# Retention scales one step later, next projections bank by bank, four row reads from GpSimd, router tables behind the first reload

## The reference, cut to what matters

```python
def first_block(x, ...):
    xn = rmsnorm(h, attn_norm_g[l])
    proj = xn @ w_in[l]
    q_da, k_da, v_da, q_r, k_r, v_r, g_r = jnp.split(proj, IN_SPLITS, axis=-1)
    o_da = diff_attention(...)
    o_r = retention(q_r, k_r, v_r, g_r)
    h = h + jnp.concatenate([o_da, o_r], axis=-1) @ w_out[l]
    xn = rmsnorm(h, ffn_norm_g[l])
    h = h + hier_moe(xn, router_group_w[l], router_group_b[l], ...)
    ...

def retention(q, k, v, g):
    s = jnp.einsum('bnchd,bnshd->bnhcs', qc, kc) * intra_decay
    intra = jnp.einsum('bnhcs,bnshe->bnche', s, vc)
    kv = jnp.einsum('bnshd,hs,bnshe->bnhde', kc, k_decay, vc)
    def step(state, kv_n):
        return state * chunk_decay + kv_n, state
    ...
    cross = jnp.einsum('bnchd,hc,bnhde->bnche', qc, q_decay, prev)
    o = head_rmsnorm(intra + cross)
    o = jax.nn.silu(g) * o

def conformer_conv(x, w_in, b_in, conv_w, conv_b, ln_g, ln_b, w_out, b_out):
    a, g = jnp.split(x @ w_in + b_in, 2, axis=-1)
    h = a * jax.nn.sigmoid(g)
    h = lax.conv_general_dilated(h, conv_w[:, None, :], ..., padding=[(30, 0)],
                                 feature_group_count=D_MODEL) + conv_b
    h = jax.nn.silu(layer_norm(h, ln_g, ln_b))
    return h @ w_out + b_out
```

## Time and profile before

| | us |
|---|---|
| median of 3 runs | 2126.69 |
| lowest, highest | 2125.68, 2127.67 |
| the profiled execution | 2125.95 |
| its span, from first to last instruction | 2124.1 |
| TensorE busy | 1962.6 (92% of the span) |
| VectorE, ScalarE, GpSimd busy | 1600.2, 1056.4, 542.0 |
| mean granted TensorE clock | 0.971 |

### The profile page before, as it was taken

One profiled execution on the slowest core, in us unless ns is written; L12 is line 12 of the kernel. 1 busy time (PEld: TensorE's weight loads), 2 busy tenths in 40 slices (PEclk: granted clock), 3 DMA queues, 4 the chain that ended last, 5 costly groups with the idle time before them and its releaser, 6 DMA issues. The chain is left out here.

```text
span 2124.1 us, 30096 instructions
## 1 busy us (share of the span) xinstructions
PE 1962.6 (92%) x11159; PEld 1057.4 (50%) x11159; DVE 1600.2 (75%) x1704; ACT 1056.4 (50%) x1396; POOL 542.0 (26%) x343
## 2 busy tenths in 40 slices
PE   6988988889499999999995899949999999999999
PEld 5775446644345544445442556534544444444444
DVE  6855637753789999999997746575697888889876
ACT  5332326731368888888875546474332323232320
POOL 2221131000023333333320001012002665557530
PEclk9999999999799999999997999979999999999999
DMA  6111320033289999999997446437101112121111
GB/s 243 41 41 40 109 60 1 1 135 127 78 328 416 403 421 404 404 398 395 407 366 303 162 161 225 148 109 287 40 1 55 65 40 79 39 79 39 61 58 80
DMA packets 80980, 363.69 MB, mean 171 GB/s; under 512 B 13993, under 2 KB 27945, under 8 KB 48313
## 3 DMA queue, kind: packets, MB, share of 16 engines
q1 hardware_dynamic: 61704, 309.64, 37.2%
q0 software_dynamic: 18640, 52.53, 7.3%
q10 hardware_dynamic: 544, 0.26, 0.0%
HBM read 337.21 MB, written 37.75 MB: 177 GB/s over the span
## 5 line engine op out<-in xcount | busy, mean ns | idle before, releaser
L432 PE MATMUL ps<-split,xt 128*128 128x512 f16 (+1 forms) x776 | 290.6, 374 | 5.2 <-issue 4.6
L649 DVE SCALAR_TENSOR_TENSOR split<-stage,split 128x2048 f16<-128x2048 f32 x128 | 289.5, 2282 | 5.6 <-ACT split L645 3.8
L433 PE MATMUL ps<-split,xt 128*128 128x512 f16 (+1 forms) x776 | 290.5, 374 | 0.0
L434 PE MATMUL ps<-split,xt 128*128 128x512 f16 (+1 forms) x776 | 290.2, 374 | 0.0
L645 ACT ACTIVATE split<-stage 128x2048 f16<-128x2048 f32 x128 | 240.5, 1904 | 94.9 <-PE ps L434 94.9
L1393 POOL TENSOR_TENSOR stage<-stage 128x1024 f32<-128x1024 f32 x48 | 134.1, 2793 | 266.8 <-DVE split L857 264.0
L432 PE MATMUL ps<-xt,split 128*128 128x512 f16 (+1 forms) x528 | 189.6, 359 | 10.0 <-issue 8.3
L433 PE MATMUL ps<-xt,split 128*128 128x512 f16 (+1 forms) x528 | 189.7, 359 | 0.0
L434 PE MATMUL ps<-xt,split 128*128 128x512 f16 (+1 forms) x528 | 189.7, 359 | 0.0
L649 DVE SCALAR_TENSOR_TENSOR arena<-arena 128x2048 f16<-128x2048 f32 x64 | 146.2, 2284 | 3.1 <-ACT arena L645 3.1
L852 ACT ACTIVATE split<-stage 128x1024 f16<-128x1024 f32 x56 | 57.3, 1048 | 143.3 <-PE pt L434 73.0
(11 more groups left out here) (541 smaller groups left out, 4805.4 us busy)
## 6 DMA issues: line engine op xcount, KB each, us to landing
stage<-in_w_gate SPq DMA_DIRECT2D x64, 1024.0 KB, 7.5
stage<-in_w_up SPq DMA_DIRECT2D x64, 1024.0 KB, 7.8
arena<-in_w_down SPq DMA_DIRECT2D x64, 1024.0 KB, 7.9
stage<-in_w_mlp SPq DMA_DIRECT2D x32, 1024.0 KB, 4.9
stage<-in_w_dense_a SPq DMA_DIRECT2D x16, 1024.0 KB, 8.7
arena<-in_conv_taps POOLq DMA_DIRECT2D x22, 640.0 KB, 5.3
stage<-in_w_dense_b SPq DMA_DIRECT2D x12, 1024.0 KB, 11.6
resid<-in_x SPq DMA_DIRECT2D x16, 512.0 KB, 5.0
```

The source lines that it names most:

```text
L432: nc.tensor.matmul(out_ap, lh, rh, start=start, stop=False)
L433: nc.tensor.matmul(out_ap, lh, rl, start=False, stop=False)
L434: return nc.tensor.matmul(out_ap, ll, rh, start=False, stop=stop)
L649: nc.vector.scalar_tensor_tensor(out=wlo(s), in0=wstage(s), scalar=WS, in1=whi(s), op0=ALU.mult, op1=ALU.subtract).then_inc(s_wo[s], 1)
```

## The change

It has three parts.

1. **Retention.** VectorE does mix(n-2) where it did mix(n-1): its order is masked(n), update(n-1), mix(n-2). The key transposes go to the right half of the bank `PS[2 par]` instead of `PT[par]`, and scores(n) no longer waits for the state. TensorE's `seven(3)` starts when all masks, seven of the eight states and six of the eight mixes are done; its products n = 1 to 3 with f = 1, which write `PT` banks 1 to 3, wait for the last state and for mixes 6, 7 and 8.
2. **Convolution.** The last four row reads of tile 7 are issued by GpSimd, ahead of the last tap load and behind its wait for the taps of load 28. They count on `s_zp[1]` instead of `s_rb[7]`, so all counts on these two are rewritten.
3. **Router tables.** SyncE requests router weights, biases and gain behind the first of the eight reloads of `x`, not behind the last.

The diff, without the renaming of one semaphore and the rewritten counts of three waits:

```diff
-        def rows_in(eng, k, groups):
+        def rows_in(eng, k, groups, landed):
             for q in groups:
                 src = u_rows[k, CG * q:CG * q + CG, :].rearrange("c (s x) -> s c x", s=PH)
-                eng.dma_start(U4[:, PH * k + q, :], src).then_inc(s_rb[k], 16)
+                eng.dma_start(U4[:, PH * k + q, :], src).then_inc(landed, 16)
...
+        def written(k):
+            return 16 * (k // 2 + 1 + 4 * (k % 2))
...
                 sp.wait_ge(s_tr, TT + t + 1)
                 sp.dma_start(H[:, t, :], a["x"][t]).then_inc(s_x[t], 16)
-            sp.dma_start(rw, a["router_w"]).then_inc(s_router_w, 16)
-            sp.dma_start(rb, a["router_b"].to_broadcast([P, NG + NE])).then_inc(s_router_w, 16)
-            sp.dma_start(gb[:, :], a["gains"][1:2, :].to_broadcast([P, D])).then_inc(s_gain, 16)
+                if t == 0:
+                    sp.dma_start(rw, a["router_w"]).then_inc(s_router_w, 16)
+                    sp.dma_start(rb, a["router_b"].to_broadcast([P, NG + NE])).then_inc(s_router_w, 16)
+                    sp.dma_start(gb[:, :], a["gains"][1:2, :].to_broadcast([P, D])).then_inc(s_gain, 16)
...
                 if j >= 3:
                     pool.wait_ge(s_cwo, 2 * j - 4)
+                if j == NCG // 2 - 1:
+                    pool.wait_ge(s_rb[7], 16)
+                    rows_in(pool, 7, range(4, PH), s_zp[1])
                 pool.dma_start(wst[j % 3], a["conv_taps"][j]).then_inc(s_cw[j % 3], 16)
...
-                    if (k, i) == (6, 1):
-                        act.wait_ge(s_rb[7], 16)
-                        rows_in(act, 7, range(4, PH))
...
-                nc.vector.tensor_tensor(ktok[par], PT[:, par, 0:256], kdec, ALU.mult)
+                nc.vector.tensor_tensor(ktok[par], PS[:, 2 * par, 256:512], kdec, ALU.mult)
...
-            for n in range(TT + 1):
+            for n in range(TT + 2):
                 if n < TT:
                     masked(n)
-                if n:
+                if 1 <= n <= TT:
                     update(n - 1)
-                    mix(n - 1)
+                if n >= 2:
+                    mix(n - 2)
...
+                        if (c, f) == (3, 1) and 1 <= n <= 3:
+                            pe.wait_ge(s_rst, TT)
+                            pe.wait_ge(s_rmix, TT - 3 + n)
...
                 if n >= 2:
                     pe.wait_ge(s_rm, n - 1)
-                    pe.wait_ge(s_rst, n - 1)
...
-                    i = nc.tensor.transpose(PT[:, par, t * P:(t + 1) * P], KR[:, t, blk], ident)
+                    i = nc.tensor.transpose(PS[:, 2 * par, 256 + t * P:384 + t * P], KR[:, t, blk], ident)
...
             pe.wait_ge(s_rm, TT)
-            pe.wait_ge(s_rst, TT)
-            pe.wait_ge(s_rmix, TT)
+            pe.wait_ge(s_rst, TT - 1)
+            pe.wait_ge(s_rmix, TT - 2)
             seven(3)
...
-                pe.wait_ge(s_rb[k], 16 * (PH + 1))
+                pe.wait_ge(s_rb[k], 16 * (PH + 1 if k < 7 else 5))
+                if k == 7:
+                    pe.wait_ge(s_zp[1], 16 * 4)
```

More of the change, by code:

```diff
@@ L361, in build @@
         s_rb = [sem(f"conv_rows_moved{k}") for k in range(KT)]
-        s_zp = [sem(f"conv_rows_written{k}") for k in range(2)]
+        s_zp = [sem(f"conv_rows_by_pool{k}") for k in range(2)]
         s_cf = sem("conv_full")
@@ L1202, in phased @@
                 sp.wait_ge(s_rb[k], 16)
-                rows_in(sp, k, range(PH if k < 7 else 4))
+                rows_in(sp, k, range(PH if k < 7 else 4), s_rb[k])
             for k in range(4):
@@ L1214, in _ @@
             for k in range(KT):
-                sp.wait_ge(s_zp[k % 2], 16 * (k // 2 + 1))
+                sp.wait_ge(s_zp[k % 2], written(k))
                 rows_back(sp, k, range(4 if k == 0 else 5), s_rb[k])
@@ L1378, in rows_last @@
             def rows_last(k):
-                pool.wait_ge(s_zp[k % 2], 16 * (k // 2 + 1))
+                pool.wait_ge(s_zp[k % 2], written(k))
                 if k >= 2:
@@ L1771, in _ @@
                 if k >= 2:
-                    act.wait_ge(s_zp[k % 2], 16 * (k // 2))
+                    act.wait_ge(s_zp[k % 2], written(k - 2))
                 nc.scalar.activation(ZN[:, k % 2, :, 0:MC], Y4[:, k, :, :], ACT.Copy).then_inc(s_ch, 1)
@@ L2852, in _ @@
             for k in range(KT):
-                pe.wait_ge(s_rb[k], 16 * (PH + 1 + (5 if k else 4)))
+                pe.wait_ge(s_rb[k], 16 * ((PH + 1 if k < 7 else 5) + (5 if k else 4)))
                 pe.wait_ge(s_cw[k % 2], 16 * pool_reads(k))
```

## The result

| | before | after |
|---|---|---|
| median, us | 2126.18 (4 runs, 2125.08 to 2127.67) | 2108.14 (4 runs, 2107.00 to 2112.43) |
| profiled execution, its span | 2125.95, 2124.1 | 2107.00, 2105.2 |
| TensorE busy | 1962.6 (92%) | 1959.5 (93%) |
| mean granted clock | 0.971 | 0.972 |

The ratio is 0.9917, with a 95% interval of 0.9905 to 0.9929. The medians differ by 18.0 us, the spans by 18.9; forecast were 17.2 and 2109.5 us, in a range of 2105 to 2114. TensorE's busy time fell by 3 us only, so most of what went is time in which it stood.

The account below looks back on a forecast made before the run. TensorE, busy 92% of the span, was taken as the bound, its idle and lower-clock time as winnable. 7.5 + 1.7 + 4.6 + 1.7 + 1.7 = 17.2 us takes 2125.95 to 2108.75, median 2109.5, range 2105 to 2114.

Parts of the forecast that it names:

- The wait of the scores goes, and the scaling closes a new circle: Retention loop: scores run beside the update, output heads wait for the scaling; update to update 4.4 us against 4.72.
- The next projections start without a gap, and their bank waits cost nothing: End of retention: next projections start at 181.0, not 188.49, and nobody waits for banks; 7.5 us with the loop.
- Half clock behind the gap, 1.7: Start of next projections: without the 3.09 us gap the clock does not fall, 1.7 us more.
- Rival A: Behind retention and the reload of x: clock not given back, 1.7 us each, 2111.2 to 2112.9; chance 0.20.
- Router, 4.6 + 1.7: Reload of x: early tables end TensorE's 4.6 us wait, and the clock dip behind it, 1.7 us, goes.
- Rival C: Behind the output projection: reloads, first gathers or weight loads take the 4.6 back, 2114.1, with the dip 2115.8; chance 0.04.
- Row reads, 1.7: Convolution tile 7: GpSimd's last read, issued 1.7 us later, lands after 3.3 us, at 1398.8 not 1400.47; 1.7 us won.
- Rival B: Convolution tile 7: GpSimd's reads land as late after issue as ScalarE's, 6.64 us; 3.4 us less, 2112.9; chance 0.11.
- Rival D: Retention loop shorter than reckoned, bound by VectorE's round of 3.9 us; 2106.5; chance 0.05.
- E: Expert stage turns from TensorE to DMA, taking 560 us, 20 more; whole kernel 2129, slower than before; chance 0.04.
- F: Retention loop: the new link costs 0.3 us or more above its price, loop stays at 4.72; 2111.4; chance 0.06.
- What passed to the end: Behind each changed place engines wait only for each other and loads they release, so all 17.2 us reach the end.

Follow-up runs that it names:

- c1_reads_behind_taps: Changed kernel, but GpSimd issues the last tap load ahead of the four row reads of tile 7; 2111.65 us (1 run).
- c2_taps_behind_rows: Changed kernel, but ScalarE issues the four reads and GpSimd holds the last tap load until all tile 7 rows have landed; 2110.56 us (1 run).
- g1_mix_first: Changed kernel, but VectorE scales the block before last ahead of the state update; 2103.62 us, ratio to before 0.9887.
- h1_early_reads: g1_mix_first, plus GpSimd's four reads of tile 7 issued ahead of the last tap load but one; 2102.67 us, ratio to before 0.9888.
- h2_five_reads: h1_early_reads, but SyncE issues three of the eight tile 7 reads and GpSimd five; 2104.22 us, ratio to before 0.9895.

## Why the prediction was right, point by point

- **The wait of the scores goes, and the scaling closes a new circle.** Right, with the output heads waiting for the last scaling. Sized 4.4 and measured 4.27: from 175.37 to the output heads at 177.55 it is 2.18, and not the 2.37 of VectorE's 0.46 + 0.43 + 0.21 + 1.13 and TensorE's wake-up of 0.14. The overlap is 0.10 and the wake-up 0.05 (scalings end at 177.50). Over six steps this is 0.8, and with it, and 0.17 by which the first product starts ahead of the modelled end of the last outputs, 7.5 became 8.49. The sum had also taken the half clock at 158 to be gone from the loop. It was, but by luck: c1_reads_behind_taps and c2_taps_behind_rows, with the same loop, have one at 149 and need 36.3 instead of 34.9.
- **The next projections start without a gap, and their bank waits cost nothing.** Right: no bracket behind 179.44, though VectorE's last scaling waits 1.60 us for the root and ends at 184.7.
- **Half clock behind the gap, 1.7.** Right, 1.69. Rival A is out for the two places it named, by fourteen kernels.
- **Router, 4.6 + 1.7.** Right: 6.49, and 6.41 alone. Rival C is out.
- **Row reads, 1.7.** The mechanism of the load behind the reads was right (landing 2.65 against 3.3 supposed), and so the wait fell to 5.57 instead of the 6.0 forecast. But the step "landed 1.7 earlier, so 1.7" failed. The half clock began 4.2 us after TensorE had stopped before, 4.4 after, and lasted 6.8 us in both, from 1397.0 to 1403.8 and from 1379.4 to 1386.2. Ending the wait sooner puts more of tile 7 under it: 5.6 us instead of 3.3, which costs half of the difference, 1.1 to 1.2. In all kernels tile 7 takes 7.6 to 7.7 us plus half of what of the half clock lies on it. So 2.14 became 1.04. I had held the clock's fall as a price per gap, all or nothing.
- **Rival B** took the landing of 6.64 to stay, so that the move would cost 1.7. It was 2.65, and even with the tap load ahead of the reads (c1_reads_behind_taps) it was 4.36 and the wait 7.73, as long as before: the move by itself costs nothing.
- **Rival D** (3.9 per step) is what g1_mix_first does, at 3.79. **E** didn't come: the experts' stretch did not move. **F** is out.
- **What passed to the end:** all, but the quiet stretch adds or takes up to 4 us in any single execution, which no term of the sum held. That it came to 0.6 here was luck, and the range should hold it.
- **The sum.** The parts were forecast at 17.2 us and gave 17.7: the loop 1.0 more and the router 0.2 more, the row reads 0.7 less. The hit within 1.4 us of the median thus owes something to errors that cancel, and to a loop without half clock, as said above.

## What to carry to other kernels

When a wait is taken out of a loop of two engines, write down both rounds, the circle through both and each engine's own, and try where the work that fills the gap stands: here the order masked, scaling, update is worth 0.5 us a step more than masked, update, scaling. When small reads end a stall, look first at which large load is queued beside them, and hold that back, before changing the engine that issues. A pause that is made shorter but not removed, with the clock falling in it, needs a price of its own: here 2.14 us less of wait were worth 1.04, since the half clock stayed as long, and 1.32 less were worth 2.15, when the half clock became half as long.

## What the hardware showed that I had not expected

- **Row reads from GpSimd land sooner after their issue than from ScalarE or SyncE.** The last read takes 2.65 against 4.56 us with the tap load behind it, 4.36 against 6.64 beside it, but GpSimd's is issued later. In h1_early_reads, where the issues lie within 0.3 us of each other, SyncE's fourth read takes 4.05 us and none of GpSimd's more than 2.9. The DMA queues of the two kernels (packets, MB, share of 16 engines), 14 us around the reads, before and after:

```profile
q0 software_dynamic: 298, 1.35, 31.8%
...
q10 hardware_dynamic: 543, 0.26, 6.7%
```

```profile
q0 software_dynamic: 485, 1.61, 35.5%
```

The same four reads (0.26 MB) are 543 packets in ScalarE's queue and 187 more in GpSimd's. That fewer, larger packets are the reason wasn't tested; h2_five_reads, where shifting a fifth read to GpSimd brought nothing to the wait, speaks against counting on a gain.

- **How long the half clock lasts.** Behind waits of 5.4 to 7.8 us for tile 7 it lasted 6.8 us in twelve kernels, behind 4.25 and 4.29 us it lasted 3.4 in two.
